# Output projection of a hybrid trunk layer: group A's units one row tile ahead of group B's, a third x buffer, and w_out of group B split behind the second softmax

## What is computed

```python
h = rms_norm(x, mix_norm_g)
u_a, v_a, q, k, v = split(h @ w_in)
y_a = gelu(u_a) * (W_s @ layer_norm(gelu(v_a)) + b_s)   # group A: 4 heads, W_s 128x128, block-lower-triangular
y_b = window_sink_attention(q, k, v, sinks, rel_bias)   # group B: 8 heads of 64, window 128, chunks of 64
x = x + concat(rms_norm(y_a), rms_norm(y_b)) @ w_out
h = rms_norm(x, ffn_norm_g)
x = x + (silu(h @ w_gate) * (h @ w_up)) @ w_down        # FFN width 2816
return rms_norm(x, final_norm_g)
```

## Time and profile before

| | |
|---|---|
| median of 3 runs | 977.4 us (977.25 to 979.72) |
| the profiled execution | 978.75 us, its span 976.9 us |
| PE busy | 942.1 us, 96% of the span |
| DVE, ACT, POOL busy | 544.7 us (56%), 391.3 us (40%), 321.0 us (33%) |
| chain that ended last | PE 91%, DVE 3%, issue 2%, ACT 2% |

### The profile page before, as it was taken

The page is one execution under the profiler, slowest core; times in us unless marked ns, Lnnn a source line. Parts: engine busy times, 40 slices in busy tenths (PEclk is TensorE's granted clock), DMA queues, the critical chain, the costliest instruction groups (busy, mean ns, idle before and its releaser), DMA issues.

```text
span 976.9 us, 11935 instructions
## 1 busy us (share of the span) xinstructions
PE 942.1 (96%) x4363; PEld 776.7 (80%) x4363; DVE 544.7 (56%) x719; ACT 391.3 (40%) x776; POOL 321.0 (33%) x343
## 2 busy tenths in 40 slices
PE   4999999969999999999999999999999999999997
PEld 3888888857788778878888888888888888888885
DVE  4660553255666797375474563663655767446653
ACT  5432332345564372243242333332433555444351
POOL 3220001001010548557566475485483200000022
PEclk9999999979999999999999999999999999999999
DMA  8320232301123253453652653644625996655543
GB/s 282 108 60 22 73 78 76 87 1 65 65 96 116 71 162 113 167 183 101 212 181 78 209 165 111 215 137 144 192 88 198 369 388 200 193 193 193 195 143 137
DMA packets 129631, 143.35 MB, mean 147 GB/s; under 512 B 15832, under 2 KB 92196, under 8 KB 129572
## 3 DMA queue, kind: packets, MB, share of 16 engines
q1 hardware_dynamic: 127968, 141.06, 44.1%
q10 hardware_dynamic: 1604, 1.52, 0.5%
HBM read 102.05 MB, written 40.50 MB: 146 GB/s over the span
## 4 chain that ended last, share of the span: by engine, by line
PE 91%; DVE 3%; issue 2%; ACT 2%; DMA 1%; POOL 1%; SPq 0%; DVEq 0%; POOLq 0%; ACTq 0%
PE ps L639 29%; PE ps L641 29%; PE ps L640 29%; DMA wv_raw<-in_w_in 1%; PE ps L832 1%; PE ps L760 1%; PE ps L772 1%; PE ps L707 1%; PE ps L650 1%; ACT S L1081 1%; DVE woB_lo L1510 0%; PE ps L715 0%; PE ps L782 0%; DVE P_lo L1577 0%; DVE B L1539 0%
## 5 line engine op out<-in xcount | busy, mean ns | idle before, releaser
L1577 DVE TENSOR_TENSOR P_lo<-P_raw,P_hi 128x512 fp32r<-128x512 f32 x132 | 134.8, 1050 | 97.1 <-POOL P_raw L576 66.8
L639 PE MATMUL ps<-T_hi,P_hi 128*128 128x512 f32 x352 | 137.0, 389 | 1.7 <-issue 1.7
L640 PE MATMUL ps<-T_lo,P_hi 128*128 128x512 f32 x352 | 136.9, 389 | 0.0
L641 PE MATMUL ps<-T_hi,P_lo 128*128 128x512 f32 x352 | 136.9, 389 | 0.0
L588 POOL TENSOR_TENSOR wd<-wd 128x256 f32<-128x256 f32 x88 | 77.8, 884 | 132.0 <-DMA wd<-in_w_down 126.8
L639 PE MATMUL ps<-rb_hi,ra_hi 128*128 128x512 f32 x308 | 119.8, 389 | 0.0
L640 PE MATMUL ps<-rb_lo,ra_hi 128*128 128x512 f32 x308 | 119.8, 389 | 0.0
L641 PE MATMUL ps<-rb_hi,ra_lo 128*128 128x512 f32 x308 | 119.8, 389 | 0.0
L1254 ACT ACTIVATE G<-G 128x512 f32<-128x512 f32 x33 | 20.9, 633 | 208.0 <-DVE G L1627 208.0
L1263 ACT ACTIVATE ra_hi<-ra 128x512 fp32r<-128x512 f32 x77 | 48.7, 632 | 102.2 <-DMA rb<-w_down_T 58.6
L511 POOL TENSOR_SCALAR small<-small 128x1 f32<-128x1 f32 (+1 forms) x17 | 9.9, 580 | 232.4 <-ACT ps L1109 135.5
(11 more groups left out here) (188 smaller groups left out, 1975.2 us busy)
## 6 DMA issues: line engine op xcount, KB each, us to landing
wd<-in_w_down SPq DMA_DIRECT2D x44, 256.0 KB, 3.6
w_down_T<-wd SPq DMA_DIRECT2D x22, 512.0 KB, 3.2
ra<-act_S SPq DMA_DIRECT2D x44, 256.0 KB, 2.6
rb<-w_down_T SPq DMA_DIRECT2D x44, 256.0 KB, 3.0
act_S<-Q SPq DMA_DIRECT2D x33, 256.0 KB, 4.9
ra<-act_A SPq DMA_DIRECT2D x33, 256.0 KB, 4.7
rb<-in_w_down SPq DMA_DIRECT2D x33, 256.0 KB, 6.1
P_raw<-in_w_gate SPq DMA_DIRECT2D x22, 256.0 KB, 4.0
```

The costliest lines, as they stand in the source:

```text
L639: mm(dst, lhs[0], rhs[0], start=start, stop=False, skip_group_check=onto)
L640: mm(dst, lhs[0], rhs[1], start=False, stop=False, skip_group_check=onto)
L641: return mm(dst, lhs[1], rhs[0], start=False, stop=stop, skip_group_check=onto)
L1577: tt(w_l[p, m][:], src[:], w_h[p, m][:].bitcast(F32), ALU.subtract).then_inc(w_split, 1)
```

## The change

PE's order is as follows now: units (r + 1, 0) and (r + 1, 1) of group A run in round r, together with (r, 2) and (r, 3) of group B; a table `OUT` gives each unit its number, from which the banks and the waits follow. In round 0 PE has three A units ahead of `probs_T(1, 0)`. `xr` has three buffers, the third at 26 KB, where A11x lay; A11x and its two loads are gone, and the sums S2 and S3 read P1's raw tile. `woB_piece` comes after the second softmax on ScalarE and DVE. At the end `h2_transposed(6, .)` comes behind all units, and `h2_transposed(7, .)` behind the first P2 product; POOL does three of the eight sums before the root of row tile 6 and the others behind it, in another order; DVE's and ScalarE's orders are adapted.

The diff, cut to its core (left out are the same replacements of `r % 2` by `r % 3` and of `4 * r + n` by `out_at` elsewhere, and indentations that follow from them):

```diff
-    xr = [at(f"xr{s}", 160 + 4 * s, [P, D]) for s in range(2)]
+    xr = [at(f"xr{s}", a, [P, D]) for s, a in enumerate((160, 164, 26))]
...
-    A11x = [at(f"A11x{m}", 26 + 2 * m, [P, 4, P]) for m in range(2)]
...
-    SUM_AT = [[("S1", 0), ("S2", 0), ("S4", 0), ("S1", 1), ("S2", 1), ("S4", 1), ("S3", 0), ("S3", 1)],
-              [(n, m) for n in ("S1", "S2", "S3", "S4") for m in range(2)]]
+    SUMS = [(n, m) for n in ("S1", "S2", "S3", "S4") for m in range(2)]
+
+    OUT = [(0, 0), (0, 1)] + [u for r in range(T - 1) for u in ((r + 1, 0), (r + 1, 1), (r, 2), (r, 3))] + [(T - 1, 2), (T - 1, 3)]
+
+    def out_at(r, n):
+        return OUT.index((r, n)) + 1
...
             sp.wait_ge(item_split, NI)
             for i in range(2):
                 sp.dma_start(xr[i][:], xt[i]).then_inc(xr_in[i], 16)
+            sp.wait_ge(unit_done, NQ1)
+            sp.dma_start(xr[2][:], xt[2]).then_inc(xr_in[2], 16)
...
             for r in range(T):
-                sp.wait_ge(out_added, 4 * r + 4)
-                sp.dma_start(x2_dram.ap()[r], xr[r % 2][:]).then_inc(x2_stored[r % 2], 16)
-                if r + 2 < T:
-                    sp.wait_ge(x2_stored[r % 2], 16 * (r // 2 + 1))
+                sp.wait_ge(out_added, out_at(r, 3))
+                sp.dma_start(x2_dram.ap()[r], xr[r % 3][:]).then_inc(x2_stored[r % 3], 16)
+                if r + 3 < T:
+                    sp.wait_ge(x2_stored[r % 3], 16 * (r // 3 + 1))
                     sp.wait_ge(x2n_ready, r + 1)
-                    sp.dma_start(xr[r % 2][:], xt[r + 2]).then_inc(xr_in[r % 2], 16)
+                    sp.dma_start(xr[r % 3][:], xt[r + 3]).then_inc(xr_in[r % 3], 16)
                 if r == 3:
                     sp.wait_ge(logits_done, HT)
                     for m in range(2):
                         weights(0, "A11", m)
-                        weights(0, "A11", m, extra=True)
                 if r == 5:
...
-                if r == 6:
                     sp.wait_ge(pv_done, T)
                     for m in range(2):
                         weights(0, "A12", m)
...
+            for r in range(T):
+                pool.wait_ge(yb_squared, r + 1)
+                root(ssqB[:, r:r + 1], msB[:, r:r + 1], rB[:, r:r + 1], DA, msB_ready, rB_ready, r + 1)
+                if r == T - 1:
+                    pool.wait_ge(out_done, out_at(T - 1, 1))
+                    for n, m in SUMS[:3]:
+                        w_sum(0, n, m)
+                if r >= 1:
+                    pool.wait_ge(x2_sq, r)
+                    root(ssq2[:, r - 1:r], ms2[:, r - 1:r], rstd2[:, r - 1:r], D, ms2_ready, rstd2_ready, r)
+            for n, m in SUMS[3:5]:
+                w_sum(0, n, m)
...
-            pool.wait_ge(out_done, 4 * T - 2)
-            for n, m in SUM_AT[0][:6]:
+            for n, m in SUMS[5:]:
                 w_sum(0, n, m)
             pool.wait_ge(x2_sq, T)
             root(ssq2[:, T - 1:T], ms2[:, T - 1:T], rstd2[:, T - 1:T], D, ms2_ready, rstd2_ready, T)
-            for n, m in SUM_AT[0][6:]:
-                w_sum(0, n, m)
...
             def out_unit(r, n):
-                u = 4 * r + n
+                u = out_at(r, n) - 1
...
                 pe.wait_ge(x2n_ready, r + 1)
                 b = 7
                 if r == T - 1 and kh:
-                    pe.wait_ge(out_added, 4 * T - 2)
+                    pe.wait_ge(out_added, out_at(T - 2, 3))
                     b = 2
...
             out_unit(0, 0)
+            out_unit(0, 1)
             yb_rows(0)
-            probs_T(1, 0)
-            out_unit(0, 1)
-            probs_T(1, 1)
-            logits(2)
-            values(1)
-            out_unit(0, 2)
-            yb_rows(1)
-            out_unit(0, 3)
-            for r in range(1, T):
+            for r in range(T):
+                if r == 0:
+                    out_unit(1, 0)
                 if r + 1 < T:
                     probs_T(r + 1, 0)
-                out_unit(r, 0)
+                if r and r + 1 < T:
+                    out_unit(r + 1, 0)
                 if r + 1 < T:
                     probs_T(r + 1, 1)
                 if r + 2 < T:
                     logits(r + 2)
-                out_unit(r, 1)
-                h2_transposed(r - 1, 0)
                 if r + 1 < T:
+                    out_unit(r + 1, 1)
+                    if r:
+                        h2_transposed(r - 1, 0)
                     values(r + 1)
-                h2_transposed(r - 1, 1)
+                    if r:
+                        h2_transposed(r - 1, 1)
                 out_unit(r, 2)
                 if r + 1 < T:
                     yb_rows(r + 1)
                 out_unit(r, 3)
+            h2_transposed(T - 2, 0)
+            h2_transposed(T - 2, 1)
...
                         product(i, p, m)
-                    if i == 0 and p == "P1":
-                        h2_transposed(T - 1, 0)
-                        h2_transposed(T - 1, 1)
+                        if i == 0 and p == "P2" and m == 0:
+                            h2_transposed(T - 1, 0)
+                            h2_transposed(T - 1, 1)
...
-            for t in range(G):
-                woB_piece(t)
             yb_to_sbuf(0)
             for _half in probabilities(1):
                 pass
+            for t in range(G):
+                woB_piece(t)
...
-                if r == T - 1:
-                    T2_hi(0)
-                    T2_hi(1)
-                    weight_hi(0, "P2", 0)
-                    weight_hi(0, "P2", 1)
-                    T2_hi(2)
-                    weight_hi(0, "P6", 0)
+            T2_hi(0)
+            T2_hi(1)
+            weight_hi(0, "P2", 0)
+            weight_hi(0, "P2", 1)
+            h2_split(T - 2, 0)
             x2_square(T - 1)
+            h2_split(T - 2, 1)
+            weight_hi(0, "P6", 0)
             weight_hi(0, "P6", 1)
+            T2_hi(2)
...
-                u, h = 4 * r + n, n % 2
+                u, h = out_at(r, n) - 1, n % 2
...
             def weight_lo(i, p, m):
                 dve.wait_ge(w_hi_ready, split_at(i, p, m))
-                if p == "P1" and i:
+                if p == "P1":
                     dve.wait_ge(w_summed, summed_at(i, "S3", m))
...
-            for t in range(G):
-                woB_piece(t)
             add_bias(1)
             maxima(1)
             yb_lo(0)
+            add_out(0, 0)
             normal_probs(1)
+            add_out(0, 1)
+            add_out(1, 0)
+            for t in range(G):
+                woB_piece(t)
             for r in range(T):
                 if r:
                     norm_x2(r - 1)
-                add_out(r, 0)
-                if r == 0:
-                    add_out(r, 1)
+                if r and r + 1 < T:
+                    add_out(r + 1, 0)
                 if r + 2 < T:
                     add_bias(r + 2)
                     maxima(r + 2)
-                if r:
-                    add_out(r, 1)
-                if r:
-                    h2_lo(r - 1, 0)
                 if r + 1 < T:
+                    add_out(r + 1, 1)
+                    if r:
+                        h2_lo(r - 1, 0)
                     yb_lo(r + 1)
-                if r:
-                    h2_lo(r - 1, 1)
+                    if r:
+                        h2_lo(r - 1, 1)
                 add_out(r, 2)
                 if r + 2 < T:
                     normal_probs(r + 2)
-                if r == T - 2:
-                    weight_lo(0, "P1", 0)
-                    weight_lo(0, "P1", 1)
                 if r == T - 1:
                     T2_to_lo(0)
                     T2_to_lo(1)
+                    weight_lo(0, "P1", 0)
+                    weight_lo(0, "P1", 1)
                 add_out(r, 3)
+            weight_lo(0, "P2", 0)
+            weight_lo(0, "P2", 1)
+            h2_lo(T - 2, 0)
+            norm_x2(T - 1)
+            h2_lo(T - 2, 1)
+            weight_lo(0, "P6", 0)
+            weight_lo(0, "P6", 1)
             T2_to_lo(2)
-            weight_lo(0, "P2", 0)
-            norm_x2(T - 1)
-            weight_lo(0, "P2", 1)
-            weight_lo(0, "P6", 0)
...
-                    weight_lo(0, "P6", 1)
                     T2_to_lo(HT - 1)
```

60 lines of the change are left out of this document (25 added, 35 removed).

## The result

Over 20 runs of each in turn, the changed kernel took 980.79 us (median, 978.05 to 982.87) and the kernel before 979.37 (976.72 to 981.75): 1.0018 of its time, 95% interval 1.001 to 1.0027, so 1.8 us more by the ratio (1.4 by the medians). The forecast was 2.1 more; both are under the 0.3% that the prediction takes for no change, though the interval leaves out 1. (Its 979.5 us were made on the 977.4 of three runs; with 979.37 in twenty, all stands 2 us higher, and 980.79 lies inside its range.) The profiled execution has a span of 978.9 us (forecast 979.0) against 976.9.

What follows compares the result with a forecast made beforehand. PE (TensorE), busy 942.1 of 976.9 us, bounds the kernel, so only its gaps and half-clock stretches count. Early -9.2 and late +11.3 give +2.1 us on the 977.4 median: 979.5 us, range 975.0 to 983.5.

Steps and rivals of the forecast that it cites:

- Early place: Start of the output projection: PE gaps of 0.65, 0.9 and 0.75 us replace 11.5 us of gaps and clock; 9.2 gained.
- The cover of woB_lo: Round 0: woB_lo ends on DVE at 210.4, unit (0,2) needs it at 212.7; hidden by 2.3 us of PE work.
- Rounds 1 to 5: Middle of the output projection: same units, waits and DVE order, 16.66 us per round; no change.
- Late place: End of the projection, counted from round 6's first transpose: 15.6 us late total against 4.3 before; 11.3 us lost.
- The 0.75 us gap: Before h2_transposed(6, 0): PE waits for DVE's norm of x2, done at R + 21.2; 0.75 us.
- the 9.0 one: Before h2_transposed(6, 1): PE waits for h2_lo(6, 0) behind eight DVE steps; 9.0 us where 1.50 stood.
- the half clock behind it: After the 9.0 us gap PE runs at half clock for one transpose group and a product: 2.24 us.
- My bound from below: If DVE and POOL did not disturb each other, h2_lo ends at R + 26.5: gap 4.9 us.
- P6 and P5: First-strip products after tile 7's transposes: gap 0.8 us before P6, and 2.8 before P5 for 1.74.
- The w_down sums: Rival: POOL's w_down sums fall on T2, P4 and P5 lo parts; up to 3.5 us, +3, total 982.5; chance 0.18.
- The full clock without disturbance: Rival: DVE and POOL disturb each other little, clock does not fall; 973.2, half of it 976.3; chance 0.21.
- The early gap: Rival: woB behind the softmax only moves the gap, round 1 starts late; 2 to 4.9 us back, 983; chance 0.06.

Runs made afterwards that it cites:

- run 4: Kernel before, with only woB moved behind the second softmax on ScalarE and DVE, order of units unchanged: 0.9977 of the kernel before.
- run 2: Changed kernel with h2_lo(6, 0) moved on DVE from behind the two P2 lo parts to directly behind add_out(7, 2): 0.9982 of the kernel before.
- run 3: The kernel of run 2 with the two P1 lo parts also ahead of the two T2 lo parts on DVE: 0.9939 of the kernel before.
- run 5: Changed kernel with the first eight weight sums on POOL replaced by zero fills: 0.9969 of the kernel before.
- run 1: The changed kernel again, unedited, on another chip group: 1.0027 of the kernel before.
- run 6: Changed kernel with h2_transposed(7, 0) and (7, 1) back behind P1's second product, ahead of both P2 products: 0.9976 of the kernel before.
- run 12: Changed kernel with only the first w_down load moved later, behind the loads of the next strip's A12: 1.0033 of the kernel before.
- run 9: Changed kernel with the edits of run 7 and run 8, and new late orders on POOL, DVE and PE: 0.9908 of the kernel before.
- run 10: The kernel of run 9 with two more exchanges of adds and lo parts on DVE, and h2_transposed(7) ahead of both P2 products: 0.9906 of the kernel before.
- run 7: The kernel of run 3 with the T1 lo part ahead of P5's second lo part on DVE: 0.9927 of the kernel before.
- run 8: Changed kernel with yb_square(0) between woB_hi copies, add_out(1, 0) behind woB_lo, logits(2) between tile 1's two probs_T: 1.0009 of the kernel before.

## Why the prediction was right

The forecast came out by its own steps, and mostly term by term, though not every one; that the sum came so close is in part luck, as said below.

*Early place.* Gap 0.65 became 0.71, 0.9 became 0.78, and 0.75 before round 1 became 0.2 (PE was free at 219.0 and not at 218.65; the softmax came at 219.19 for 219.4). Gained: 11.5 - 1.7 = 9.8 us for the forecast's 9.2. The cover of woB_lo held: it ended at 210.2, needed at 212.87. Run 4 shows that the move of woB alone does not close the gap.

*Rounds 1 to 5*: nothing, as said.

*Late place.* Counted from round 6 (302.55), x2n was there at 21.1 (forecast 21.2), and h2_transposed(6, 1) began at 30.3 (30.6). The 0.75 us gap was 0.51, the 9.0 one 8.57, the half clock behind it 2.05 for 2.24 (transposes and product took 338.14 - 332.89 = 5.25, where 0.45 + 2.75 is usual). Runs 2 and 3 show that DVE's order makes the gap, run 5 that 5.0 of the 9.1 us are POOL's sums. My bound from below, 4.9 without any disturbance, stands beside 4.07 measured; it still charged P2's lo parts with waits for the sums.

The Trainium skill's rule (SBUF — State Buffer, § Who interferes with whom), that a VectorE instruction with two SBUF inputs and a GpSimd read exclude each other, gave h2_lo's end at R + 31.5. Measured: 30.2. A pair beside two sums took 2.76 us against 1.28 beside none, so the rule's direction holds here, but the single file was packed closer than its single lengths.

*P6 and P5.* Forecast 0.8 and 2.8, measured 1.39 and 2.43 (1.78 and 1.90 in run 1); the sum 3.6 against 3.8 and 3.7. Run 6 shows the cause to be the seam, as the term had it. From ScalarE's T2_hi to P5 it was 10.56 us (346.36 to 356.92) for the 10.1 taken over from before; that half microsecond is the w_down sums.

*What failed.* The term for P5 had no half clock behind it: 1.6 us that were not in the sum. Without them the measured terms are 0.51 + 8.57 + 2.05 + 1.39 + 2.43 = 14.95 us late, 10.6 lost against 9.8 gained, so 0.8 where the forecast had 2.1. By the rows themselves P5 starts 161.29 us behind unit (0, 0) for 160.33 before, 0.96 later. The missing 1.6 us brought it back: 2.4 by the gaps, 2.2 by the spans from unit (0, 0), 1.8 by the runs. Two errors of opposite sign met there, and that is luck; with either error alone the total would still have stayed inside the stated range.

*The rivals.* The w_down sums did fall on T2 lo, P4 lo and P5 lo (347.05 for 4.50 us on POOL), so the mechanism was there, but its price was wrong: 0.59 us before P5, a third of a microsecond of it already in the gap before P6, where I had 3.5 (rows at run 12). I put all of DVE's longer work on a path that ScalarE sets. Reading what ends DVE's own wait in that row would have told. The forecast had these sums at nothing. The full clock without disturbance did not come; half clock stood behind every gap of that length. The early gap closed.

What stays open: the worth of T1 lo forward, and of the three early gaps, each about 1 us by ratios whose intervals overlap; and why the stretch behind P5 differs by some 2 us from trace to trace.

## What to carry to other kernels

Work that is taken ahead leaves the end of its stage without cover: ask which waits that work had hidden there, and place them anew in the same change. In a queue written by hand, what PE waits for now goes ahead of what it needs in 5 us; one moved line gave 3.5 us here and two gave 7.7. And when each removed gap comes back a few instructions later, look whether the engine in front is simply busy: moving on then gained nothing here (runs 9 and 10), while taking other work away from beside it did shorten what it had to do (11.4 to 6.8 us in run 5). An edit that only moves the disturbing work shows no more than its new place (run 12).

## What the runs showed of the hardware that I had not expected

The half clock also follows short gaps, and not always the same ones. It came behind the gaps of 8.57, 6.18, 4.07, 3.73, 3.45, 2.98, 2.95 and 2.43 to 2.45 us in every trace that had them. Behind 1.50, 1.90 and 1.94 it came in one trace each (runs 3, 1 and 7); behind 1.50 and 1.74 in the kernel before, 1.50 in run 7, 1.84 and 1.88 in run 2, 1.86 and 1.89 in run 8 and 1.93 in run 9 it did not. Runs 3 and 7 have the same code up to their 1.50 us. Where worked out it cost 1.45 us (run 10) to 2.05. So two executions of one kernel can differ by that much with the same gaps, and a single trace is not enough to price an edit of 2 us.
